# Up products with joined convolution rows, last rows by ScalarE, down weights issued ahead, and low parts shared four to three between GpSimd and VectorE

## The chip, the cores and the metric

The kernel runs on one core of a Trainium2 chip, in one launch. TensorE multiplies, VectorE, ScalarE and GpSimd do elementwise work, and SyncE (SP) issues most of the DMA transfers. The metric is the device time in microseconds, as the median of some runs; lower is better.

## What is computed

One layer of a decoder for 512 prompt tokens and 8 sequences of 8 sample tokens, 576 columns T in all, 2048 features, in fp32. The change lies in its last part, the gated MLP with a causal convolution of three taps over the tokens:

```python
def _ffn(u_hist, lp):
    uc = _dwconv_valid(u_hist, lp['w_dw_f'], lp['b_dw_f'])     # 3 taps a channel, 2 * 5632 channels
    gate, val = jnp.split(uc, 2, axis=-1)
    return jnp.dot(jax.nn.silu(gate) * val, lp['w_down'])

    u = jnp.dot(h2, lp['w_up'])                                # 2048 -> 2 * 5632
    u_hist = jnp.pad(u, ((0, 0), (FFN_CONV_W - 1, 0), (0, 0))) # a sample sequence: its saved rows
    y = x1 + gt2 * _ffn(u_hist, lp)
    return y, (k, v, ki, a_hist[:, -(CONV_W - 1):], u_hist[:, -(FFN_CONV_W - 1):])
```

The last two rows of u of each sequence are outputs too.

## The kernel before

Every fp32 matrix product is made of three fp32r products: a weight tile is split into a high part (ScalarE rounds it, `whi`) and a low part (the weight less the high part, `wlo`), the other operand as well (`XH`, `XL`), and TensorE adds high × high, high × low and low × high. A matmul takes a 128 x 128 weight and 288 columns (`TH`, half of T).

**Up loop.** The 44 pairs of channel tiles (gate and value; `FT` = 44) go in order. The first two pairs are ordinary products. The other 42 (`NU`) are the turns of a loop in which two inner halves by two halves of the columns by two channel tiles are made with seven products instead of eight (a Strassen-like scheme), from sums and differences of the weight blocks (`add_forms` 1 to 4, on VectorE, into `sums` and `raw`) and of the operand (four forms, `b11` to `b22`, made once on VectorE, split by `form_rows` on ScalarE and `form_lo` on VectorE). Turn i makes pair f = i + 2. A product p has two halves h of four weight tiles, 12 matmuls each.

For each half, ScalarE's `form_hi` writes `whi`, then a low part follows, then TensorE's `product`. There are four half buffers, so the high part of a half waits until TensorE is done with the half four before it. Before the change GpSimd makes the low parts of products 0, 2, 3, 5 and 6 (`POOL_LO`, two pieces of 256 columns a half, L925) and adds `u2` at the end (L929); VectorE makes those of products 1 and 4 (`DVE_LO`, L2595, 512 columns at once). The result of a pair comes from the seven products by adds on VectorE (`late_sum`, `gate_rows`, `value_rows`), with copies by ScalarE (`snap`), into rows `up` (prompt, two zero columns ahead) and `us` (sample, two saved rows ahead of each sequence).

**Convolution.** ScalarE makes the first tap with the bias (`taps`, L1272 prompt, L1273 sample), VectorE the other two (`conv3`, L2553 to L2558, prompt and sample apart), with copies of the last rows between (L2555, L2556). ScalarE applies silu, VectorE multiplies gate and value (`gate`, L2566), and the product goes to DRAM (`g_far`). A pair's convolution runs in the turn after its products.

**Loads.** SP's queue loads four raw blocks of 512 KB a turn, in the order 3, 2, 0, 1 (`block`), each when its slot is free. After the last turn four blocks of down weights, the residual `x1T` (in two pieces) and the first gated tiles `g32` are loaded the same way, and the down loop follows: 88 units of 48 matmuls, with low parts by GpSimd (L933) and `residual` on VectorE.

Each engine runs its instructions in the order in which the code is written; waits are semaphores.

## Time and profile before

| | us |
|---|---|
| median of 3 runs | 3043.79 (3033.14 to 3053.01) |
| profiled execution | 3037.9 |
| its span, first to last instruction | 3035.6 |
| TensorE busy in the span | 2802.8 (92%) |
| VectorE, ScalarE, GpSimd busy | 1986.6, 1081.7, 1688.1 |
| up loop after its first turn | 1457 to 2445 |

A row of the page's first part gives an engine's busy time, its share and its instructions. A row by stage gives the busy time of each engine in a stretch. A row of a timeline or of the chain gives start, duration, engine and line; in brackets how long the engine sat idle before it and who released it. A row of one line gives the fastest, the median and the slowest duration of its instructions. PE is TensorE, DVE VectorE, ACT ScalarE, POOL GpSimd.

### The profile page before, as it was taken

The page shows a single profiled execution, that of the slowest core. Times are in us where ns is not written, and L with a number is a line of the kernel's source. Part 1 is how long each engine was busy: PE and PEld are TensorE (multiplying, and loading weights), DVE is VectorE, ACT ScalarE, POOL GpSimd, SP SyncE. Part 2 cuts the span into 40 slices and gives each one's busy share as a digit, 9 for nine tenths or more (in the row PEclk, how much of TensorE's full clock was granted, in tenths as well). Part 3 has the DMA queues.
Part 4 walks back from the last instruction along what each step waited for, and adds up shares of the span by engine and source line. Part 5 has one row for each costly group of instructions (what it writes and reads, how often), then busy time and mean ns, then how long its engine had stood idle before and what let it go on. Part 6 is the DMA issues. An engine that isn't in the chain of part 4 may idle for free.

```text
span 3035.6 us, 52988 instructions
## 1 busy us (share of the span) xinstructions
PE 2802.8 (92%) x20368; PEld 2537.7 (84%) x20368; DVE 1986.6 (65%) x3277; ACT 1081.7 (36%) x1924; POOL 1688.1 (56%) x1936
## 2 busy tenths in 40 slices
PE   5798899999989779988999999999999989999999
PEld 2296588889955559988999999999999989999998
DVE  2225379999867542238898889888888854444442
ACT  2212323332125331226445555555555532121212
POOL 0134344443330254457888888888888854545453
PEclk9899999999989989999999999999999999999999
DMA  9822155552268763341333333333333353332323
GB/s 291 272 80 80 51 178 172 182 160 60 78 202 291 223 213 116 114 133 39 96 108 106 101 97 96 100 101 108 105 101 97 97 201 115 99 112 97 115 84 97
DMA packets 473891, 391.94 MB, mean 129 GB/s; under 512 B 29385, under 2 KB 402789, under 8 KB 473061
## 3 DMA queue, kind: packets, MB, share of 16 engines
q1 hardware_dynamic: 462882, 363.24, 39.1%
q0 software_dynamic: 8704, 19.27, 2.0%
q10 hardware_dynamic: 2075, 6.34, 0.7%
q8 instruction: 147, 2.41, 0.3%
q14 instruction: 83, 0.67, 0.1%
HBM read 363.85 MB, written 25.66 MB: 128 GB/s over the span
## 4 chain that ended last, share of the span: by engine, by line
PE 57%; POOL 20%; DVE 12%; issue 4%; DMA 3%; ACT 2%; ACTq 0%; SPq 0%; POOLq 0%; DVEq 0%
PE ps L1973 16%; POOL wlo L925 16%; PE ps L1425 16%; PE ps L2005 14%; DVE yb L2271 3%; DVE ye L2274 3%; DMA raw<-in_w_ada 2%; PE ps L1459 2%; POOL wlo L933 2%; DVE prod L2255 1%; POOL u L929 1%; ACT whi L1290 1%; DVE scP L2182 1%; PE ps L1837 1%; PE ps L1591 1%
## 5 line engine op out<-in xcount | busy, mean ns | idle before, releaser
L925 POOL TENSOR_TENSOR wlo<-raw,whi 128x256 fp32r<-128x256 f32 x672 | 707.7, 1084 | 103.5 <-ACT whi L1290 103.5
L876 POOL TENSOR_TENSOR wlo<-raw,whi 128x256 fp32r<-128x256 f32 (+1 forms) x424 | 350.1, 856 | 491.0 <-ACT whi L978 491.0
L2005 PE MATMUL ps<-XH,whi 128*128 128x288 f32 x1344 | 404.4, 301 | 56.3 <-POOL wlo L925 56.3
L933 POOL TENSOR_TENSOR wlo<-raw,whi 128x256 fp32r<-128x256 f32 x352 | 274.7, 812 | 295.8 <-ACT whi L1314 295.8
L1425 PE MATMUL ps<-XH,whi 128*128 128x288 f32 (+1 forms) x1760 | 390.4, 303 | 7.4 <-POOL wlo L876 6.0
L2005 PE MATMUL ps<-XH,wlo 128*128 128x288 f32 x1344 | 396.9, 295 | 0.0
L2005 PE MATMUL ps<-XL,whi 128*128 128x288 f32 x1344 | 396.8, 295 | 0.0
L2005 PE MATMUL ps<-x1R,whi 128*128 128x288 f32 x1344 | 395.6, 294 | 0.0
L1425 PE MATMUL ps<-XL,whi 128*128 128x288 f32 (+1 forms) x1760 | 379.0, 296 | 0.0
L1425 PE MATMUL ps<-XH,wlo 128*128 128x288 f32 (+1 forms) x1760 | 378.6, 297 | 0.0
L1290 ACT ACTIVATE whi<-raw 128x512 fp32r<-128x512 f32 x420 | 264.1, 629 | 235.2 <-PE ps L2005 223.1
L2481 DVE TENSOR_TENSOR yS<-ps,adaT 128x64 f32<-128x64 f32 x192 | 42.9, 224 | 421.9 <-PE ps L1973 330.3
L2005 PEld LDWEIGHTS ps<-XH,whi 128*128 128x128 f32 x1344 | 252.6, 188 | 74.8 <-issue 47.6
L1425 PEld LDWEIGHTS ps<-XH,whi 128*128 128x128 f32 (+1 forms) x1760 | 283.6, 190 | 26.7 <-issue 15.1
L978 ACT ACTIVATE whi<-raw 128x1024 fp32r<-128x1024 f32 (+1 forms) x106 | 111.0, 1051 | 525.5 <-PE ps L1425 358.9
L1425 PEld LDWEIGHTS ps<-XH,wlo 128*128 128x128 f32 (+1 forms) x1760 | 284.7, 190 | 0.0
L1425 PEld LDWEIGHTS ps<-XL,whi 128*128 128x128 f32 (+1 forms) x1760 | 284.2, 189 | 0.0
L2005 PEld LDWEIGHTS ps<-x1R,whi 128*128 128x128 f32 x1344 | 255.5, 190 | 0.0
L2005 PEld LDWEIGHTS ps<-XL,whi 128*128 128x128 f32 x1344 | 253.1, 188 | 0.0
L1314 ACT ACTIVATE whi<-raw 128x1024 fp32r<-128x1024 f32 x88 | 93.5, 1062 | 447.6 <-PE ps L1973 436.8
L2005 PEld LDWEIGHTS ps<-XH,wlo 128*128 128x128 f32 x1344 | 252.2, 188 | 0.0
L1459 PE MATMUL ps<-raw,sums 128*32 128x512 f32 x768 | 152.3, 671 | 37.9 <-DMA raw<-in_w_ada 37.7
(384 smaller groups left out, 6369.1 us busy)
## 6 DMA issues: line engine op xcount, KB each, us to landing
raw<-in_w_ada SPq DMA_DIRECT2D x192, 512.0 KB, 4.8
raw<-in_w_up SPq DMA_DIRECT2D x176, 512.0 KB, 4.2
raw<-in_w_down SPq DMA_DIRECT2D x88, 512.0 KB, 3.4
raw<-in_w_in SPq DMA_DIRECT2D x68, 512.0 KB, 5.6
Vp<-in_cache_v POOLq DMA_DIRECT2D x128, 128.0 KB, 3.9
raw<-in_w_out SPq DMA_DIRECT2D x32, 512.0 KB, 3.9
raw<-in_cache_k SPq DMA_DIRECT2D x64, 128.0 KB, 2.3
g32a<-g_far SPq DMA_DIRECT2D x6, 1152.0 KB
```

Of the source, the lines that this page charges most:

```text
L876: last = G.tensor_tensor(l[:, a:a + width // 4], raw_of(u, m)[:, a:a + width // 4], h[:, a:a + width // 4].bitcast(F32), ALU.subtract)
L925: last = G.tensor_tensor(lp[:, a:a + 256], src[:, a:a + 256], hp[:, a:a + 256].bitcast(F32), ALU.subtract)
L933: last = G.tensor_tensor(wlo[:, d % 2, a:a + 256], raw[:, d % 4, a:a + 256], whi[:, d % 2, a:a + 256].bitcast(F32), ALU.subtract)
L978: A.activation(parts(u, m)[0][:, 0:width], raw_of(u, m)[:, 0:width], ACT.Copy)\
L1290: A.activation(w_half(whi, i, p, h), form_of(p)[:, h * 512:h * 512 + 512], ACT.Copy).then_inc(s_hi, 1)
L1314: A.activation(whi[:, d % 2, :], raw[:, d % 4, :], ACT.Copy).then_inc(s_hi, 1)
L1425: ins = mm(dst[:, t, :], wt, x(k0 + k, t), start=st, stop=sp_)
L1459: ins = mm(ps_all[g:g + 32, bk, :], csT[:, kt, :], raw[:, s, kt % 2 * 512:kt % 2 * 512 + 512], start=kt < 4, stop=kt >= KT - 4)
L1973: ins = mm(pair(2 if nn else 6)[:, t, :], wt, x[g % 2][:, k, t * TH:t * TH + TH], start=k == 0 and wt is hp and x is gH, stop=k == GT - 1 ...
L2005: ins = mm(dst, wt, x(4 * h + k), start=h + k == 0 and wt is a and x is xh, stop=h == 1 and k == 3 and wt is b)
L2271: STT(even, hist[:, k:k + SEQ], w_tap(i, k), even, ALU.mult, ALU.add).then_inc(s_pe_, 1)
L2274: STT(odd, hist[:, k:k + SEQ], w_tap(i, k), odd, ALU.mult, ALU.add).then_inc(s_po, 1)
```

## The change

The prompt and sample rows of a channel tile now lie in one row `cin` of 594 columns, and the convolution's result in one row `conv` of 592, so that each tap is one instruction over all of it (the columns between sequences are computed and not used). The copies of the last rows go from VectorE to ScalarE. VectorE also makes product 6's low parts and the `u2` add; GpSimd keeps products 0, 2, 3 and 5. The four operand forms stand behind the first pair's convolution and gate. After the last turn the four blocks of down weights are issued ahead of `x1T`, which is loaded in four pieces.

```diff
-        POOL_LO, DVE_LO = (0, 2, 3, 5, 6), (1, 4)
+        POOL_LO, DVE_LO = (0, 2, 3, 5), (1, 4, 6)
...
+        CV = 2 + SEQ + DB * (2 + DS)
+        cin = at(o_f, "cin", [128, 2, CV])
+        up = cin[:, :, 0:2 + SEQ]
+        us = cin[:, :, 2 + SEQ:].rearrange("p v (b t) -> p v b t", b=DB)
+        conv = [four[:, v * CV:v * CV + CV - 2] for v in range(2)]
...
             last = NU - 1
             g_in(0, product_done(last, 1))
-            block(NU, 0)
-            sp.wait_ge(*product_done(last, 3))
+            for s in (3, 2, 0, 1):
+                block(NU, s)
+            for a in range(4):
+                x1_in(a, product_done(last, 4))
+                if a == 0:
+                    g_out(FT - 2)
             g_in(1, product_done(last, 3))
-            x1_in(1, product_done(last, 3))
-            block(NU, 1)
-            x1_in(0, product_done(last, 4))
-            block(NU, 2)
-            block(NU, 3)
-            g_out(FT - 2)
...
-                pool.wait_ge(*s_q.at(i + 1))
-                pool.wait_ge(*s_snap.at(2 * i + 2))
-                G.tensor_tensor(u2[:, :], u2[:, :], p5[:, :], ALU.add).then_inc(s_u4.sem, 1)
...
             def taps(f, v):
                 ch = f + v * FT
-                if v == 1:
-                    w(act, s_gt, f)
+                w(act, s_gt, f)
                 bias, tap = vT[:, 2, ch:ch + 1], vT[:, 5, ch:ch + 1]
-                A.activation(tmp[:, v, 0:SEQ], up[:, v, 0:SEQ], ACT.Identity, bias=bias, scale=tap)
-                A.activation(by8(tmp[:, v, SEQ:T]), us[:, v, :, 0:DS], ACT.Identity, bias=bias, scale=tap).then_inc(s_t0, 1)
+                A.activation(conv[v], cin[:, v, 0:CV - 2], ACT.Identity, bias=bias, scale=tap).then_inc(s_t0, 1)
+                last_rows_of(f, v)
+
+            def last_rows_of(f, v):
+                g, j, par = f // GT, f % GT, f // GT % 2
+                if j == 0:
+                    w(act, s_fot, g - 1)
+                A.activation(uS[:, par, v * GT + j, :].rearrange("p (b r) -> p b r", r=2), us[:, v, :, DS:], ACT.Copy)
+                A.activation(uP[:, par, v * GT + j, :], up[:, v, SEQ:], ACT.Copy).then_inc(s_us.sem, 1)
...
-                link.hold(STT(pa, up[:, v, 1:1 + SEQ], tap(1), pa, ALU.mult, ALU.add))
-                link(STT(sa, us[:, v, :, 1:1 + DS], tap(1), sa, ALU.mult, ALU.add))
-                V.tensor_copy(uS[:, par, v * GT + j, :].rearrange("p (b r) -> p b r", r=2), us[:, v, :, DS:])
-                V.tensor_copy(uP[:, par, v * GT + j, :], up[:, v, SEQ:])
-                STT(pa, up[:, v, 2:2 + SEQ], tap(2), pa, ALU.mult, ALU.add)
-                STT(sa, us[:, v, :, 2:2 + DS], tap(2), sa, ALU.mult, ALU.add).then_inc(s_c3, 1)
+                link(STT(conv[v], cin[:, v, 1:CV - 1], tap(1), conv[v], ALU.mult, ALU.add))
+                STT(conv[v], cin[:, v, 2:CV], tap(2), conv[v], ALU.mult, ALU.add).then_inc(s_c3, 1)
...
-                TT(gout[f % 2], sq[:, 0, :], tmp[:, 1, :], ALU.mult).then_inc(s_gt, 1)
+                TT(gout[f % 2][:, 0:SEQ], conv[0][:, 0:SEQ], conv[1][:, 0:SEQ], ALU.mult)
+                TT(by8(gout[f % 2][:, SEQ:T]), sample[0], sample[1], ALU.mult).then_inc(s_gt, 1)
...
                     TT(up[:, 0, 2:2 + TH], p1[:, :], bank(7, 128, 0, TH), ALU.add).then_inc(s_c11.sem, 1)
+                    TT(u2[:, :], u2[:, :], p5[:, :], ALU.add).then_inc(s_u4.sem, 1)
...
             conv3(0, 0)
             conv3(0, 1)
             gate(0)
+            operand_forms()
             add_forms(0, 1)
...
                 late_sum(i)
                 gate_rows(i)
+                lo(i, 6)
                 gate(f - 1)
                 if i < NU - 1:
                     add_forms(i + 1, 1)
...
-            for a in range(2):
-                dve.wait_ge(*s_x1i[a].at(16))
             for g in range(NG):
                 for n in range(16):
+                    if g == 0 and n % 4 == 0:
+                        dve.wait_ge(*s_x1i[n // 4].at(16))
```

On VectorE, the stretch of a turn from the gate rows to the two weight sums for products 3 and 2, before (`wlo<-sums` here is product 1's low part, `tmp` and `sq` the convolution's rows):

```order
L2612 TENSOR_TENSOR up<-up,ps 128x288
L2566 TENSOR_TENSOR rstd<-sq,tmp 128x576
L2575 TENSOR_TENSOR sums<-raw 128x1024
L2618 TENSOR_TENSOR up<-p1,ps 128x288
L2595 TENSOR_TENSOR wlo<-sums,whi 128x512 x2
L2622 TENSOR_TENSOR up<-u2,ps 128x224
L2623 TENSOR_TENSOR us<-u2,ps 128x8x8
L2579 TENSOR_TENSOR raw<-raw 128x1024
L2583 TENSOR_TENSOR raw<-sums,raw 128x1024
```

And in the changed kernel, with `four` for the convolution's rows:

```order
L2612 TENSOR_TENSOR cin<-cin,ps 128x288
L2595 TENSOR_TENSOR wlo<-sums,whi 128x512 x2
L2565 TENSOR_TENSOR four<-four 128x512
L2566 TENSOR_TENSOR four<-four 128x64
L2575 TENSOR_TENSOR sums<-raw 128x1024
L2618 TENSOR_TENSOR cin<-p1,ps 128x288
L2619 TENSOR_TENSOR u2<-u2,p5 128x288
L2595 TENSOR_TENSOR wlo<-sums,whi 128x512 x2
L2623 TENSOR_TENSOR cin<-u2,ps 128x224
L2624 TENSOR_TENSOR cin<-u2,ps 128x8x8
L2579 TENSOR_TENSOR raw<-raw 128x1024
L2583 TENSOR_TENSOR raw<-sums,raw 128x1024
```

Product 6's two low parts have come in ahead of the gate, the gate is two instructions, and `u2` stands ahead of product 1's low parts.

In SP's queue, from the last up weights to the down loop's first loads, before:

```order
L804 DMA g32a<-g_far 128x4x576
L792 DMA raw<-in_w_down 128x4x256
L804 DMA g32b<-g_far 128x4x576
L809 DMA x1T<-x1_far 128x8x576
L792 DMA raw<-in_w_down 128x4x256
L809 DMA x1T<-x1_far 128x8x576
L792 DMA raw<-in_w_down 128x4x256 x2
L797 DMA g_far<-sq 128x576
```

And in the changed kernel:

```order
L807 DMA g32a<-g_far 128x4x576
L795 DMA raw<-in_w_down 128x4x256 x4
L812 DMA x1T<-x1_far 128x4x576
L800 DMA g_far<-four 128x576
L812 DMA x1T<-x1_far 128x4x576 x3
L807 DMA g32b<-g_far 128x4x576
```

All four weight blocks stand ahead of `x1T` now, and `g32b` behind it.

## Rows read from the trace of the kernel before

**Rows 1.** The page, part 1: busy us, share of the span, instructions.

```profile
PE 2802.8 (92%) x20368; PEld 2537.7 (84%) x20368; DVE 1986.6 (65%) x3277; ACT 1081.7 (36%) x1924; POOL 1688.1 (56%) x1936
```

**Rows 2.** By stage, up loop: length, busy PE, PEld, DVE, ACT, POOL, clock, DMA.

```profile
1457.00:2445.00 988.00, 936.56 (x6905) 918.51 (x6904) 882.46 (x1188) 506.15 (x962) 868.25 (x860) 1.00 0.35 103
```

**Rows 3.** The chain that ended last, down stage: start, us, what.

```profile
2642.88 44.70 PE ps L1973 x336
```

**Rows 4.** The chain that ended last, one turn of the up loop.

```profile
1941.60 9.84 PE ps L2005 x72
...
1952.16 5.40 POOL wlo L925 x6
...
1958.26 1.94 POOL wlo L925 x2
1960.20 0.77 POOL u L929
```

**Rows 5.** The products' line: what TensorE sat idle for, us and times.

```profile
  POOL wlo L925: 85.6, 128
```

**Rows 6.** Single lines: instructions, fastest/median/slowest ns, first and last start.

```profile
L2554 DVE SCALAR_TENSOR_TENSOR tmp<-us,vT,tmp x88: 267/755/764, 1400.2 to 2456.8; 128x64 f32<-128x64 f32 x88
...
L2555 DVE COPY uS<-us x88: 174/611/618, 1400.9 to 2457.1; 128x16 f32<-128x16 f32 x88
...
L2595 DVE TENSOR_TENSOR wlo<-sums,whi x84: 683/1086/1292, 1428.6 to 2422.6; 128x512 fp32r<-128x512 f32 x84
...
L925 POOL TENSOR_TENSOR wlo<-raw,whi x672: 719/1179/3037, 1422.1 to 2437.8; 128x256 fp32r<-128x256 f32 x168
```

**Rows 7.** Timeline of VectorE, one turn: start, us, instruction, idle time before.

```profile
1936.25 1.72 DVE L2575 TENSOR_TENSOR sums<-raw 128x1024 f32<-128x1024 f32 x1 [0.73 <-POOL wlo L925]
...
1940.87 0.38 DVE L2622 TENSOR_TENSOR up<-u,ps 128x224 f32<-128x224 f32 x1
...
1944.22 1.23 DVE L2553 SCALAR_TENSOR_TENSOR tmp<-up,vT,tmp 128x512 f32<-128x512 f32 x1
...
1951.36 1.22 DVE L2588 TENSOR_TENSOR sums<-raw 128x1024 f32<-128x1024 f32 x1
...
1957.34 0.45 DVE L2607 TENSOR_TENSOR up<-u,ps 128x288 f32<-128x288 f32 x1
1957.83 0.39 DVE L2610 TENSOR_TENSOR up<-up,p 128x224 f32<-128x224 f32 x1
...
1958.76 0.85 DVE L2566 TENSOR_TENSOR sq<-sq,tmp 128x576 f32<-128x576 f32 x1
```

**Rows 8.** Timeline of ScalarE, the same turn.

```profile
1948.81 0.20 ACT L1279 ACTIVATE us<-sF 128x16 f32<-128x16 f32 x1
...
1956.97 0.68 ACT L1325 ACTIVATE sq<-tmp 128x576 f32<-128x576 f32 x1 [1.69 <-DVE tmp L2558]
...
1958.77 1.31 ACT L1290 ACTIVATE whi<-raw 128x512 fp32r<-128x512 f32 x2 [0.58 <-DMA raw<-in_w_up]
```

**Rows 9.** Timelines of VectorE and TensorE ahead of the up loop.

```profile
1390.10 2.99 DVE L2530 TENSOR_TENSOR x1T<-x1T 128x2304 f32<-128x2304 f32 x1
...
1399.12 1.11 DVE L2553 SCALAR_TENSOR_TENSOR tmp<-up,vT,tmp 128x512 f32<-128x512 f32 x1
...
1409.87 1.20 DVE L2566 TENSOR_TENSOR sq<-sq,tmp 128x576 f32<-128x576 f32 x1
1419.58 1.23 DVE L2575 TENSOR_TENSOR sums<-raw 128x1024 f32<-128x1024 f32 x1 [8.50 <-DMA raw<-in_w_up]
...
1399.83 0.58 PE L1425 MATMUL ps<-XH,whB 128*128 128x288 f32 x1 [7.09 <-POOL wlB L876]
```

**Rows 10.** Timelines of TensorE and ScalarE where the down stage begins.

```profile
2449.09 0.82 PE L1973 MATMUL ps<-gHa,whi 128*128 128x288 f32 x2 [3.70 <-POOL wlo L933]
...
2462.33 0.82 PE L1973 MATMUL ps<-gHa,whi 128*128 128x288 f32 x2 [5.35 <-DVE x1T L2485]
...
2458.35 1.06 ACT L1314 ACTIVATE whi<-raw 128x1024 fp32r<-128x1024 f32 x1 [3.87 <-DMA raw<-in_w_down]
```

49 lines of the change are left out of this document (22 added, 27 removed).

## The prediction

> **What bounds the kernel now.** I read the busy shares and slices of the page first, then the busy time by stage, then the chain of waits inside the longest stage. Over the span TensorE is busy 92% of the time and no other engine comes near [rows 1]. By stage it is the up loop that counts: 1457 to 2445 us, 988 us for its last 41 turns (turn 0 ends at about 1457), so 24.1 us a turn, and the granted clock there is 1.00 [rows 2]. In the down stage TensorE is fed without a pause. A row of the chain there gives its pace: 44.70 us for 336 matmuls of 288 columns, 0.133 us each [rows 3]. A turn of the up loop has 168 such matmuls (7 products of two halves, 12 matmuls a half), 22.35 us. So 24.1 - 22.35 = 1.75 us of a turn is waiting, and 41 × 1.75 = 72 us is all that this loop can give.
>
> The chain through one turn says who is waited for [rows 4]: GpSimd subtracts the low part of product 6, adds u2, subtracts four pieces for product 0 of the next turn, and only then TensorE runs 72 matmuls in a row. In the list of TensorE's waits at this line GpSimd's low parts hold 85.6 us [rows 5]. GpSimd is busy 868 of 988 us [rows 2], 21.1 us a turn, and what it does not use is its own wait for the high parts.
>
> The durations of single instructions show a second thing. The same VectorE instruction on 64 columns takes 0.27 us at its fastest and 0.755 at the median; a GpSimd piece of 256 columns 0.72 and 1.18 [rows 6]. Each stays the longer by about one instruction of the other: VectorE and GpSimd hold each other up where both read SBUF, one instruction for one. A tiny instruction therefore costs VectorE as much waiting (0.49 us) as a large one. The Trainium skill (SBUF — State Buffer, section "SBUF: two separate sides") says this as a rule: the shared ports are an exclusive lock, and the loser blocks for the winner's whole instruction. The trace agrees, with the two medians just given. Without such a lock the first chain below would cost its low figure and the time would be the first rival's.
>
> **GpSimd's part.** Of its 21 instructions a turn it loses five: four pieces of product 6 and u2. By the chain that is 1.94 + 0.77 us plus two of the six pieces that take 5.40 [rows 4]: about 4.5 us off the engine that is waited for. 16 pieces at 1.18 are 18.9 us, under 22.35 even when all are held up. GpSimd's sum stops being the bound; the time until one given piece is done still can be.
>
> **VectorE's part.** It loses, for each of the two rows of channels, two 64-column taps (0.755 each) and the copy of 16 columns (0.61): 2 × 2.12 = 4.2 us a turn [rows 6]; the copies of 2 columns I leave uncounted. It gains 80 columns on each of four taps: 0.08 each from the fastest times of 512 and 64 columns (0.683 - 0.267 over 448), 0.3 together; two low parts, 0.68 alone and 1.09 at the median, 1.4 to 2.2; the u2 add, as a 224-column add of two SBUF tiles (0.39 [rows 7]) alone, 0.9 held up; the gate cut in two, 0.27 to 0.755 more. In all 2.4 to 4.2 us. From 882/41 = 21.5 us busy [rows 2] that leaves 19.7 to 21.5: no bound by sum either.
>
> ScalarE gains two copies a channel row and loses the 64-column tap; at 506 of 988 us busy [rows 2] it has room. The copies follow each tap in its order; a copy of 16 columns takes it 0.20 us [rows 8], so the next high part comes up to 0.25 us later, or no later where the tap that goes pays for them. New waits: the first row's tap now waits for the gate of the pair before, with ScalarE's high parts queued behind it; that gate is half a turn old by then, so I count nothing. The waits for x1 move into the down loop, one for each four tiles, behind loads that are cut in four; nothing either.
>
> **Which wait ends last next.** Two chains run round a turn and come back to TensorE. I hold them against the halves that TensorE has meanwhile. Nine halves are 108 × 0.133 = 14.36 us; the last result of a half is out 0.26 us later than the next half begins (9.84 us for 72 matmuls [rows 4] less 72 × 0.133), which leaves 14.1.
>
> Chain A begins when product 4 ends and must feed half 2 of product 2 of the next turn. VectorE, in its new order: the four value sums at L2607 to L2612, 1.42 (from L2607's start to the gate's [rows 7]); product 6's two low parts, 1.3, as GpSimd has nothing to do just then; the gate in two pieces, 1.7 (1.05 alone, 1.9 held up); the sum for product 1, 1.7 (1.72 [rows 7]; 1.2 alone); L2618, 0.4; u2, 0.5; product 1's low parts, 1.3 (2.2 at the median; GpSimd is now done with product 0 earlier); the last value rows and the two sums at L2579 and L2583, 3.35 (from 1940.87 to 1944.22 [rows 7]); then the two taps, each behind a GpSimd piece of product 2, 1.3 each (1.23 and 0.08); GpSimd's last piece 0.6, its start overlapped. Sum 14.9, against 14.1: 0.7 to 0.8 us short. Unheld, with 1.2 for a sum of 1024 columns and 0.8 for a tap, it is 1.42 + 1.3 + 1.05 + 1.2 + 0.4 + 0.4 + 1.3 + 0.43 + 2.4 + 1.6 + 0.72 = 12.2 and hides. Held up by each of the eight GpSimd pieces that can lie in it, it is 8 × 0.49 = 3.9 more, less the 0.49 of the last, which holds nobody: 15.7 at most.
>
> Chain B begins when product 2 ends and must feed the second half of product 0: high part 0.71 with ScalarE's 0.25 ahead of it, low part 0.69, the sum for product 6 (L2588) 1.22, and then block 0 of the next weights, which is issued behind that sum: 1952.58 to 1958.77, 6.2 us, the high part waiting for the DMA [rows 7, 8]. Then 0.71 and four GpSimd pieces, 2.9 alone or 4.7 at the median: 12.7 to 14.5, against the same 14.1. So it lies between 1.4 in hand and 0.4 short; alone it would give a little less than chain A.
>
> I take chain A's 0.7: the turn goes from 24.1 to 22.35 + 0.7 = 23.05, and TensorE's wait moves from product 0 to product 2 (or partly stays at product 0's second half). 41 turns × 1.05 = 43 us.
>
> **Into the loop.** VectorE's four operand forms now stand behind the first channel pair's taps and gate. Before, they held GpSimd's pieces up, 3.0 us for a pair of form and piece, and TensorE idled 7.09 us for them until 1399.83 [rows 9]. That goes. But the forms then meet the next eight pieces instead, and all four first loads of the loop wait in SP's queue for the last of these (VectorE sat 8.50 us for them before [rows 9]). By the same 3.0 us a pair I place this last piece so: the two pairs of taps and the gate took 1399.12 to 1411.07 before, 12 us, of which some 4.5 are small instructions and hold-ups that go; 7.5 us from about 1393.7 (1 us after TensorE's stop at 1392.74) is 1401; four forms held up at 3.0 and two more pieces at 0.72 end at 1414.5. Before, the last piece must have been out by 1419.58 less a load's 5 to 6 us (the 6.2 of chain B), so about 1414 too: nothing gained there. So the idle time moves and I count 0; both ends are +2 and -6.
>
> **Out of the loop.** Two idle stretches, 3.70 and 5.35 us [rows 10]. In the second ScalarE waited 3.87 us for the third block of down weights, whose load stood in SP's queue behind those of x1 (4.7 MB) and g. Now the four blocks stand ahead of x1. The high part of that block then no longer waits for its load but for its buffer, which TensorE frees when it stops at 2456.98; it began at 2458.35 [rows 10]. That is 1.1 us with a signal's time, and the first stretch may give 0.5 as GpSimd comes free sooner, though VectorE's subtraction for g starts later. 1.5 us; ends 0 and 6.
>
> **The sum.** The profiled execution took 3037.9 us (span 3035.6 and 2.3 around it): 3037.9 - 43 - 0 - 1.5 = 2993. The runs of before have their median 6 us above this execution and lie 10 us to either side of it, so runs of after at 2990 to 3000 would be the same statement.
>
> **Rivals.** First, both chains hide (chain A between 12.2 and 14.1): the floor, 22.35 to 22.5 a turn, 41 × 1.7 = 70 us, 2964 with the same ends. For it: GpSimd has five instructions less, so fewer VectorE instructions are held up than before. Against: my placing of the pieces meets a hold-up at nearly every large VectorE instruction.
>
> Second, the hold-ups are nearly complete: chain A 15.1 to 15.7, the turn 23.35 to 23.95, a gain of 6 to 31 us with the 1.5, 3005 to 3030; 3018 in the middle. For it: VectorE was busy 882 of 988 us [rows 2], and much of that was hold-up. Against: only eight pieces lie in the chain.
>
> Third, on the other side: VectorE's order becomes the bound. Product 6's low part now stands in VectorE's row between the value sums and the gate; it waits for ScalarE's high part, which stands behind the silu, which waits for VectorE's own second pair of taps. Whatever is late there delays the gate, the next turn's sums and both chains. VectorE needs 21.5 us if all is held up and waited 2.6 us a turn before (24.1 less 21.5); the same wait on top of it gives 24.1, and from there on it decides. With 3.7 us of waits the turn is 25.2: 41 × 1.1 = 45 us slower, 3083. Against: 2.3 us of small instructions go from each pair of taps, and ScalarE's silu waited only 1.69 us for the second pair before [rows 8].
>
> Fourth, low part 6 only changes hands: TensorE waits for VectorE at product 6 as long as it waited for GpSimd at product 0, and the time stays 3038. The value sums (1.42) and one low part (0.69) take 2.1 us, and TensorE still works two halves there, 3.19 less 0.26, so I see little for it.
>
> **Chances.** My forecast (turn 22.65 to 23.35, 2977 to 3005) 0.52; the floor 0.20; nearly complete hold-ups 0.18; VectorE the bound 0.06; unchanged 0.04. Two in ten left out give 2958 (the floor and the start's 6 us) to 3022; the likeliest case alone is 2977 to 3005. A measurement of this kernel tells about 1% from no change, 30 us. Faster by more than that, below 3013 from the median of 3044: 0.52 + 0.20 + a third of 0.18 = 0.78; within: 0.12 + 0.04 = 0.16; slower 0.06.
>
> **What the profile would show.** Right: turns of 23 us in the chain; GpSimd's pieces no longer followed by u2; TensorE's wait at product 2 or at the second half of product 0, with VectorE's sums or taps and the w_up load ahead of it; VectorE busy about 20.5 us a turn; no 7 us gap at 1393 but one of similar size before 1431; the load of the third down block landing before TensorE wants it. Wrong: waits at product 6 on VectorE's L2595, a turn over 23.6, or no wait at all.

## The result and the profile after

| | before | after |
|---|---|---|
| median of the runs, us | 3043.91 (3033.14 to 3053.01, 4 runs) | 3009.77 (3004.04 to 3014.29, 4 runs) |
| ratio, 95% interval | | 0.9888 (0.9851 to 0.9925) |
| profiled execution, us | 3037.9 | 3004.0 |
| its span, us | 3035.6 | 3001.9 |

The forecast was 2993 with a range of 2958 to 3022. The time lies 17 us above the forecast, inside the range, and the kernel is 1.1% faster.

The first part of the page of after answers [rows 1] (busy us, share of the span, instructions):

```profile
PE 2803.3 (93%) x20368; PEld 2536.7 (85%) x20368; DVE 1915.1 (64%) x3095; ACT 1080.0 (36%) x2012; POOL 1528.7 (51%) x1726
```

TensorE does the same work; VectorE is busy 71.5 us less and GpSimd 159.4 us less. The row by stage for the up loop, cut as in [rows 2] (length, busy PE, PEld, DVE, ACT, POOL, clock, DMA share, GB/s):

```profile
1457.71:2413.61 955.90, 937.98 (x6910) 919.20 (x6908) 816.87 (x1028) 505.25 (x1045) 711.15 (x654) 1.00 0.36 107
```

The 41 turns take 955.9 us where they took 988, so a turn is 23.3 us. VectorE is busy 816.87 / 41 = 19.9 us of it (21.5 before), GpSimd 17.3 (21.2 before). What TensorE sits idle for at the line of the products, the first turn included (us, times), beside [rows 5]:

```profile
  POOL wlo L926: 66.0, 128
```

This row adds up matmuls and weight loads, which the profile counts as two engines, PE and PEld. The matmuls' waits alone, of after and of before (us, times, the longest):

```profile
PE ps L2008 <- POOL wlo L926: 27.2, 45, 4.9
PE ps L2005 <- POOL wlo L925: 57.3, 84, 2.4
```

So GpSimd's low parts are still what ends last, with about half of the matmuls' idle time. The chain through one turn of after, beside [rows 4] (start, us, what):

```profile
1919.19 1.29 DVE wlo L2595 x2
...
1921.54 0.76 DVE rstd L2566
1922.30 1.71 DVE sums L2575
1924.09 0.12 ACT whi L1294
...
1924.63 0.61 ACT whi L1294
...
1926.17 0.20 ACT uS L1276
1926.37 0.09 ACT uP L1277
1926.47 0.54 ACT whi L1294
1927.07 5.36 POOL wlo L926 x4
1932.47 8.51 PE ps L2008 x60
```

Before, the chain ended in GpSimd's pieces for product 0, and TensorE then ran 72 matmuls. Now it starts with product 6's low part on VectorE, goes through the gate (L2566) and the sum for product 1 (L2575), then through **ScalarE**: product 1's high parts, the first tap and its two copies of last rows (L1276, L1277), product 2's high part. Product 2's weights are a raw block as it was loaded: no sum of VectorE's feeds them. (The two sums at L2579 and L2583 make the weights of products 4 and 3, not 3 and 2 as the section on the change has it.) GpSimd's four pieces for product 2 take 5.36 us, and TensorE starts product 2's second half at 1932.47. Beside those pieces VectorE and GpSimd work as follows in after (timelines of the two; the third column is the engine), the place of [rows 7]:

```profile
1926.47 1.21 DVE L2579 TENSOR_TENSOR raw<-raw 128x1024 f32<-128x1024 f32 x1
1927.72 1.65 DVE L2583 TENSOR_TENSOR raw<-sums,raw 128x1024 f32<-128x1024 f32 x1
1929.29 1.31 DVE L2555 SCALAR_TENSOR_TENSOR four<-cin,vT,four 128x592 f32<-128x592 f32 x1
1930.63 1.20 DVE L2556 SCALAR_TENSOR_TENSOR four<-cin,vT,four 128x592 f32<-128x592 f32 x1
1932.68 0.98 DVE L2595 TENSOR_TENSOR wlo<-raw,whi 128x512 fp32r<-128x512 f32 x1 [0.85 <-ACT whi L1294]
1935.03 1.16 DVE L2595 TENSOR_TENSOR wlo<-raw,whi 128x512 fp32r<-128x512 f32 x1 [1.37 <-ACT whi L1294]
```

```profile
1927.07 8.56 POOL L926 TENSOR_TENSOR wlo<-raw,whi 128x256 fp32r<-128x256 f32 x8 [2.47 <-ACT whi L1294]
```

GpSimd makes eight pieces without a pause, four for product 2 and four for product 3, each beside a sum, a tap or a low part of VectorE. In the turn shown TensorE waits 0.65 us at product 2's second half, 0.14 at product 3's first, and the two halves behind those waits run 0.1 us longer each. (These waits are counted from one matmul's start to the next one's, less 0.133; the profile's idle time is shorter, since the records of matmuls overlap.) It waits nowhere else: at products 0, 1, 4, 5 and 6 the low part is 0.5 us or more ahead of its half in the two turns read.

**Where the 33.7 us of span came from.** I cut both traces at the same matmuls.

| stretch | before | after | difference |
|---|---|---|---|
| up to the end of the stage's first part on TensorE | 1392.7 | 1390.5 | -2.3 |
| from there to turn 1's first product | 63.8 | 67.25 | +3.4 |
| 41 turns | 988.7 | 955.8 | -32.9 |
| last up product to the second return of TensorE | 17.1 | 14.8 | -2.3 |
| the rest | | | +0.3 |

The first row has nothing to do with the change: in the five runs below that have the forms at their old place this moment lies between 1386.4 and 1397.2 us, with the same code ahead of it. So one execution's time carries some us from there, and I compare loops by the turn's length: the mean of 40 turns in the profiled execution, 24.14 us before and 23.31 after.

### The profile page after: what moved, and what is told of

It reads as the page before. It is cut to its first block, busy times and chain, and to the rows that moved or that the text cites. A ratio compares the mean times of both kernels' runs of the same rounds, so it can differ in the third digit from the quotient of the medians.

```text
span 3001.9 us, 52583 instructions
## 1 busy us (share of the span) xinstructions
PE 2803.3 (93%) x20368; PEld 2536.7 (85%) x20368; DVE 1915.1 (64%) x3095; ACT 1080.0 (36%) x2012; POOL 1528.7 (51%) x1726
## 4 chain that ended last, share of the span: by engine, by line
PE 57%; DVE 19%; POOL 11%; issue 6%; ACT 4%; DMA 3%; ACTq 0%; SPq 0%; DVEq 0%; POOLq 0%
PE ps L1976 17%; PE ps L1428 17%; PE ps L2008 12%; POOL wlo L926 8%; DMA raw<-in_w_ada 3%; PE ps L1462 2%; DVE yb L2274 2%; DVE ye L2277 2%; DVE sums L2575 2%; ACT whi L1294 2%; DVE wlo L2595 2%; POOL wlo L931 2%; POOL wlo L877 1%; DVE prod L2258 1%; DVE scP L2185 1%
## 5 line engine op out<-in xcount | busy, mean ns | idle before, releaser
L926 POOL TENSOR_TENSOR wlo<-raw,whi 128x256 fp32r<-128x256 f32 x672 | 735.4, 1125 | 259.0 <-ACT whi L1294 259.0
L877 POOL TENSOR_TENSOR wlo<-raw,whi 128x256 fp32r<-128x256 f32 (+1 forms) x424 | 359.4, 878 | 486.2 <-ACT whi L976 486.2
L931 POOL TENSOR_TENSOR wlo<-raw,whi 128x256 fp32r<-128x256 f32 x352 | 276.3, 816 | 296.9 <-ACT whi L1318 296.9
L1428 PEld LDWEIGHTS ps<-XH,whi 128*128 128x128 f32 (+1 forms) x1760 | 282.7, 189 | 30.6 <-issue 15.7
```

What stands on the lines that cost most here:

```text
L877: last = G.tensor_tensor(l[:, a:a + width // 4], raw_of(u, m)[:, a:a + width // 4], h[:, a:a + width // 4].bitcast(F32), ALU.subtract)
L926: last = G.tensor_tensor(lp[:, a:a + 256], src[:, a:a + 256], hp[:, a:a + 256].bitcast(F32), ALU.subtract)
L931: last = G.tensor_tensor(wlo[:, d % 2, a:a + 256], raw[:, d % 4, a:a + 256], whi[:, d % 2, a:a + 256].bitcast(F32), ALU.subtract)
L1428: ins = mm(dst[:, t, :], wt, x(k0 + k, t), start=st, stop=sp_)
```

## The experiments

My theory before the runs: VectorE and GpSimd hold each other up, and the chain through VectorE's sums and taps makes GpSimd's pieces for products 2 and 3 late. Rivals: VectorE's order as a whole is the bound; ScalarE's high part of product 2, which stands behind the first tap, comes late; block 0's transfer is late. Twelve kernels, all of them changes to after. Times are medians of the runs; each ratio is taken to runs of before made together with that kernel, whose medians lie between 3039.2 and 3043.9 us.

| run | turn, us | time, us | ratio to before, 95% interval |
|---|---|---|---|
| before | 24.14 | 3043.9 | |
| after | 23.31 | 3009.8 | 0.9888 (0.9851 to 0.9925) |
| low6_pool | 23.60 | 3023.4 (one run) | |
| split_rows | 23.91 | 3032.4 (one run) | |
| lo512 | 23.75 | 3023.0 | 0.9939 (0.9920 to 0.9958) |
| tap_apart | 23.11 | 2999.5 | 0.9866 (0.9834 to 0.9897) |
| hi_ahead | 23.36 | 3011.6 | 0.9908 (0.9872 to 0.9944) |
| p3_dve | 23.37 | 3004.1 | 0.9876 (0.9852 to 0.9899) |
| p3_taps_behind | 23.74 | 3023.8 | 0.9948 (0.9927 to 0.9969) |
| p3_order | 23.07 | 2995.5 | 0.9859 (0.9838 to 0.9879) |
| p3_order_hi | 22.37 | 2968.4 | 0.9769 (0.9752 to 0.9785) |
| p3_order_taps | 22.64 | 2979.7 | 0.9812 (0.9785 to 0.9839) |
| sp_order | 23.31 | 3017.0 (one run) | |
| ends_undone | 23.31 | 3010.3 (one run) | |

### What the two halves of the change are worth: low6_pool and split_rows

Product 6's low part and u2 go back to GpSimd:

```diff
-        POOL_LO, DVE_LO = (0, 2, 3, 5), (1, 4, 6)
+        POOL_LO, DVE_LO = (0, 2, 3, 5, 6), (1, 4)
```

> The changed kernel, with product 6's low part and the addition of u2 given back to GpSimd; the joined rows, the early down weights and the ends of the stage stay. If the third low part on VectorE is worth what the prediction says, GpSimd's pieces of product 0 are late again (fourteen 1.18-1.19 us pieces... ten halves of two pieces and an addition make about 21 us behind VectorE, and block 0's transfer before them): TensorE waits at product 0 again, 1.0-2.0 us a turn, and the turn is 23.6 to 24.1 us, the time 3022 to 3042 us. If VectorE's own chain alone sets the turn (its work falls by two low parts and an addition, some 2.3 us), the turn is at most that of the changed kernel, 23.3 us or less, and the time 3010 us or less.

The turn is 23.60 us, and the chain is that of [rows 4] again:

```profile
1925.03 4.78 POOL wlo L926 x5
...
1930.63 1.89 POOL wlo L926 x2
1932.52 0.77 POOL u L930
1933.28 4.68 POOL wlo L926 x4
...
1938.01 9.84 PE ps L2011 x72
```

So the wait is back at product 0, as expected. Product 0's four pieces take what they took before (4.68 us and 4.66). What has become shorter is the stretch from product 5's first piece to product 6's second half: 5.6 us (1925.03 to 1930.63) against 6.1 (1952.16 to 1958.26). The joined rows alone are worth 24.14 - 23.60 = 0.54 us a turn, the third low part with u2 another 0.29 on top.

The other half alone: product 6 stays on VectorE, the taps are cut into prompt and sample rows and VectorE copies the last rows, as before the change:

```diff
-                link(STT(conv[v], cin[:, v, 1:CV - 1], tap(1), conv[v], ALU.mult, ALU.add))
-                STT(conv[v], cin[:, v, 2:CV], tap(2), conv[v], ALU.mult, ALU.add).then_inc(s_c3, 1)
+                link.hold(STT(pa, up[:, v, 1:1 + SEQ], tap(1), pa, ALU.mult, ALU.add))
+                link(STT(sa, us[:, v, :, 1:1 + DS], tap(1), sa, ALU.mult, ALU.add))
+                V.tensor_copy(uS[:, par, v * GT + j, :].rearrange("p (b r) -> p b r", r=2), us[:, v, :, DS:])
+                V.tensor_copy(uP[:, par, v * GT + j, :], up[:, v, SEQ:])
+                STT(pa, up[:, v, 2:2 + SEQ], tap(2), pa, ALU.mult, ALU.add)
+                STT(sa, us[:, v, :, 2:2 + DS], tap(2), sa, ALU.mult, ALU.add).then_inc(s_c3, 1)
```

> The changed kernel, with the convolution's second and third taps cut into prompt and sample rows again, and the last rows copied by VectorE; product 6's low part stays on VectorE. By the theory that VectorE and GpSimd hold each other up instruction for instruction, four sample taps and four copies a turn come back, each of up to 0.6-0.75 us whatever its size: VectorE's chain to product 2's second half grows by two sample taps and two copies (1.5 to 2.6 us), and the turn is 24.5 to 26 us, the time 3060 to 3120 us, slower than before the change. By the theory that columns set the price (the same columns in all, four short instructions at 0.15-0.25 us each), the chain grows by 0.6 to 1.0 us, the turn is 23.9 to 24.3 us, the time 3035 to 3052 us.

The single instructions cost what the theory says: 0.755 us for 64 columns and 0.612 for 16 at the median (line: fastest/median/slowest ns), and only the copy of 2 columns stays at 0.155:

```profile
L2560 DVE SCALAR_TENSOR_TENSOR four<-cin,vT,four x88: 272/755/765, 1400.9 to 2447.0; 128x64 f32<-128x64 f32 x88
L2561 DVE COPY uS<-cin x88: 174/612/618, 1401.2 to 2447.3; 128x16 f32<-128x16 f32 x88
L2562 DVE COPY uP<-cin x88: 153/155/716, 1401.3 to 2447.4; 128x2 f32<-128x2 f32 x88
```

But the turn is 23.91: below the range of the first theory, whose durations came, and at the lower end of the second's, whose durations did not. The row by stage says why:

```profile
1458.90:2439.38 980.48, 958.97 (x6910) 923.05 (x6908) 970.53 (x1356) 478.25 (x881) 689.33 (x655) 1.00 0.35 104
```

VectorE is busy 970.53 of 980.48 us (99%), 23.67 of a turn of 23.91. The small instructions add 3.75 us of work a turn to the 19.92 of after; 3.4 us of that goes into what VectorE had idle, and only the rest lengthens the turn. I had added them to the chain as if nothing in it were waiting. So here VectorE's order is the bound, the third rival of the forecast. This half of the change alone (the first tap stays joined on ScalarE, the gate cut in two) is worth 24.14 - 23.91 = 0.23 us a turn.

### How the two engines hold each other up: lo512

One subtraction of 512 columns a half on GpSimd instead of two of 256:

```diff
-                        for a in (0, 256):
-                            last = G.tensor_tensor(lp[:, a:a + 256], src[:, a:a + 256], hp[:, a:a + 256].bitcast(F32), ALU.subtract)
-                        last.then_inc(s_lo, 1)
+                        G.tensor_tensor(lp, src, hp.bitcast(F32), ALU.subtract).then_inc(s_lo, 1)
```

> The changed kernel, with each half's low part on GpSimd made by one subtraction of 512 columns instead of two of 256. In the trace of the changed kernel a 256-column piece takes 0.73 us beside an idle VectorE and 1.2 us beside a working one; a VectorE subtraction of 512 columns grows from 0.68 to 1.22 us and the 0.22 us sample gate to 0.76 us when a piece runs beside it, 0.54 us each, whatever their own size. If the hold-up is a fixed price for each instruction, it stays at 0.54 us on VectorE, a half on GpSimd costs 1.4 + 0.5 = 1.9 us instead of 2.4 us, the waits at products 2 and 3 go, and the turn is 22.4 to 22.7 us, the time 2972 to 2985 us. If the two engines take turns, each for as long as the other's instruction works, the same VectorE instructions grow by about 1.08 us (the sample gate to 1.3 us), a half costs 2.0 to 2.5 us, and only the order changes: the turn is 22.9 to 23.5 us, the time 2993 to 3018 us.

First after, then lo512, for the sample gate (fastest/median/slowest ns of 64 columns) and GpSimd's pieces:

```profile
L2566 DVE TENSOR_TENSOR four<-four x22: 220/762/766, 1399.0 to 2410.6; 128x64 f32<-128x64 f32 x22
L926 POOL TENSOR_TENSOR wlo<-raw,whi x672: 723/1187/3039, 1421.5 to 2406.6; 128x256 fp32r<-128x256 f32 x168
```

```profile
L2564 DVE TENSOR_TENSOR four<-four x22: 211/1309/1317, 1402.2 to 2428.8; 128x64 f32<-128x64 f32 x22
L925 POOL TENSOR_TENSOR wlo<-raw,whi x336: 1277/1814/3606, 1424.7 to 2421.8; 128x512 fp32r<-128x512 f32 x168
```

The gate's 64 columns take 0.22 us alone, 0.76 beside a piece of 256 columns and 1.31 beside one of 512: 0.54 and 1.09 us more. So the price is not a fixed one for an instruction. It grows with the instruction that the other engine works on, and is 0.18 or 0.19 us less than that one takes at its fastest (0.723 and 1.277). The second theory of this run is right in VectorE's durations; GpSimd's half, 1.81 us at the median, is nearer the first's 1.9 than the second's 2.0 to 2.5. The second theory's turn (22.9 to 23.5) is not right either: 23.75 us, since VectorE's instructions that meet a piece are held up twice as long, and product 6's low part on VectorE becomes late (by 0.54 us in the turn read). Small pieces are the better ones here.

### Which wait makes product 2 late: tap_apart and hi_ahead

The third tap of the value rows goes into VectorE's idle time between the two halves of product 4's low part:

```diff
-                    conv3(f - 1, 1)
+                    tap_a(f - 1, 1)
...
-                lo(i, 4)
+                lo(i, 4, 0)
+                if i:
+                    tap_b(f - 1, 1)
+                lo(i, 4, 1)
```

> The changed kernel, with the third tap of the value rows of the pair before put between the two halves of product 4's low part, where VectorE stands idle 1.4 us a turn. By the theory that GpSimd's pieces for products 2 and 3 are late because VectorE's sums and taps run beside them, one tap of 0.6-0.7 us leaves that stretch: TensorE's wait at product 2's second half falls from 0.65 to 0-0.3 us, that at product 3 from 0.35 to 0-0.2 us, the turn is 22.4 to 22.8 us and the time 2972 to 2990 us. By the rival that VectorE's order as a whole is the bound, the moved tap delays the low part of product 4's second half, and with it the next chain: the turn stays at 23.2 to 23.6 us, the time 3005 to 3022 us. By the rival that ScalarE's high part of product 2 is what comes late, nothing changes at product 2: 23.3 us, 3008 to 3012 us.

Turn 23.11, 0.2 us less; that of my theory was 22.4 to 22.8. The wait at product 2's second half fell from 0.65 to 0.12 us as expected, but one of 0.48 came at product 3's second half. The timeline of GpSimd shows eight pieces as long as before (8.56 us in after):

```profile
1926.49 8.58 POOL L926 TENSOR_TENSOR wlo<-raw,whi 128x256 fp32r<-128x256 f32 x8 [2.47 <-ACT whi L1294]
```

Taking one VectorE instruction from beside product 2's pieces only put it beside product 3's.

On ScalarE, product 2's first high part goes ahead of the first tap and its copies:

```diff
-                    first_tap(f - 1, 1)
                     form_hi(i, 2, 0)
+                    first_tap(f - 1, 1)
```

> The changed kernel, with ScalarE's high part of product 2's first half ahead of the first tap of the pair before, not behind it. If that high part, which starts about 0.65 us after its buffer could take it, is what GpSimd's piece waits for, GpSimd's pieces of products 2 and 3 come 0.4-0.65 us earlier, the wait at product 2's second half falls from 0.65 to 0-0.25 us, and the turn is 22.6 to 22.9 us, the time 2980 to 2995 us. If the pieces are late through VectorE's sums and taps alone, they finish when those do: the turn stays at 23.2 to 23.4 us, the time 3003 to 3014 us. If the tap, coming 0.6 us later, delays VectorE, the turn grows to 23.5 to 23.9 us, the time 3018 to 3034 us.

The turn is 23.36, unchanged, as the second case had it, but not for its reason. Product 2's second half now has its low part 0.14 us early and TensorE does not wait there. It waits 0.67 us at product 3's first half and 0.14 at its second:

```profile
1928.85 9.54 POOL L926 TENSOR_TENSOR wlo<-raw,whi 128x256 fp32r<-128x256 f32 x8 [1.75 <-ACT whi L1294]
```

The eight pieces start earlier and take 9.54 us. In the chain of hi_ahead no VectorE instruction is left: it goes from TensorE's release of a half buffer through one high part and six of these pieces (7.70 us) to product 3. So both single edits heal the place that the forecast named, and the run of eight pieces, four halves in a row beside working VectorE instructions, keeps the turn within 0.2 us of where it was. TensorE uses up those four halves in 4 × 12 × 0.133 = 6.4 us.

### Taking product 3 out of the run of eight: p3_dve and what stood behind it

```diff
-        POOL_LO, DVE_LO = (0, 2, 3, 5), (1, 4, 6)
+        POOL_LO, DVE_LO = (0, 2, 4, 5), (1, 3, 6)
...
-                lo(i, 4)
+                lo(i, 3)
```

> The changed kernel, with product 3's low part on VectorE and product 4's on GpSimd (VectorE still makes three of seven). In the changed kernel GpSimd has eight pieces in a row for products 2 and 3, beside VectorE's sums and taps, and they take 8.6 us; TensorE's waits there are 0.65 us at product 2 and 0.35 us at product 3. If this run of eight pieces is the bound, product 3's wait goes and product 2's, which comes ahead of it, stays: the turn is 22.9 to 23.0 us, the time 2992 to 3000 us. If what binds is VectorE's chain to the taps, product 3's low part, which now stands behind them, is late: the turn is 23.3 to 24.0 us, the time 3008 to 3040 us.

TensorE waits neither at product 2 nor at product 3 any more (the low parts are 0.7 to 2.7 us early), but the turn is 23.37: it waits at product 0. The chain there:

```profile
1914.25 4.42 POOL wlo L926 x4
...
1918.68 0.37 SPq L795
...
1919.14 5.56 DMA raw<-in_w_up
...
1924.78 0.64 ACT whi L1294
...
1925.49 4.49 POOL wlo L926 x4
...
1930.03 5.04 PE ps L2008 x36
```

Product 4 is read from block 2's buffer, GpSimd now frees that buffer 2 us later against TensorE's use of it (the low part is 1.07 us ahead of its half, 3.02 in after), and SyncE issues block 0, which is wanted first, behind block 2. This is the forecast's second chain (block 0's transfer, then GpSimd's pieces for product 0), lengthened by a queue. (Counted from a turn's first product, block 2 is issued at 14.0 us here and at 12.4 in after; the 5 to 5.6 us that two expectations below name for this compare the times of two executions.) The same with the value rows' taps behind product 3's low part, product 2's high part ahead of the tap and the operand forms at their old place:

> The changed kernel with three things: product 3's low part on VectorE and product 4's on GpSimd; the value rows' two taps behind product 3's low part instead of ahead of it; product 2's first high part ahead of the first tap on ScalarE. Also the operand forms stand ahead of the first convolutions again, as before the change. If the wait in a turn is that of GpSimd's eight pieces for products 2 and 3 beside VectorE's sums and taps, then four pieces beside the two sums, started 0.65 us earlier, end 0.2 us or more ahead of TensorE's need, VectorE's product 3 is 1.5 us ahead of it, and no wait is left: the turn is 22.35 to 22.7 us, the start some 3 us shorter, the time 2967 to 2983 us. If VectorE's total work in its order binds, the taps come later and hold the sums for product 6 and the next turn's chain: the turn is 23.2 to 23.8 us, the time 3002 to 3030 us.

Turn 23.74: product 2's second half is 1.8 us early, and TensorE waits 1.3 and 0.5 us at product 0's first half in the two turns read (0.6 on average), for block 0, and 0.5 at its second. Both turns lie in the range of the case that blamed VectorE, but VectorE's low part of product 3 is 1.8 us or more early in both, and VectorE is busy only 772 of 973 us in the second. Both expectations failed by the same omission; neither theory had the queue of loads in it.

Then block 0 ahead of block 2 in SyncE's order, with the forms at their old place:

```diff
                 block(i + 1, 3)
-                block(i + 1, 2)
+                block(i + 1, 0)
...
-                block(i + 1, 0)
+                block(i + 1, 2)
                 block(i + 1, 1)
```

> The changed kernel with product 3's low part on VectorE and product 4's on GpSimd (as in the run of that alone), SyncE's issue of block 0 ahead of that of block 2 in each turn, and the operand forms ahead of the first convolutions again. In the run with products 3 and 4 exchanged alone, the waits at products 2 and 3 went (slack 0.7 to 1.7 us) and new ones stood at product 0 (0.35 and 0.52 us): there block 2's buffer came free 5.6 us later than in the changed kernel, since GpSimd reads it now, and block 0 is issued behind it (0.47 us after block 2, at 1942.31). If that queue is the cause, block 0 goes out some 3 us earlier, product 0's waits go, and what is left is the chain from product 4's end to product 2's second half, 14.3 to 14.5 us against TensorE's 14.35: the turn is 22.35 to 22.6 us, the start some 3 us shorter, the time 2960 to 2975 us. If product 0 waits for GpSimd's own pieces (which were held to 2.2 us a half there by VectorE's gate and sum), the turn stays at 23.1 to 23.4 us, the time 2995 to 3006 us.

Product 0's wait goes (0.85 us in hand), so the queue was its cause. But the turn is 23.07, since 0.65 us at product 2's second half is back, the wait of after to the hundredth: I had taken that chain's length from a run in which TensorE waited elsewhere first. With product 2's high part ahead of the tap as well:

> The same three edits, and ScalarE's high part of product 2's first half ahead of the first tap. In the run of that edit alone GpSimd's first piece for product 2 came 0.65 us earlier against product 4's end, and the wait went from product 2 to product 3, whose pieces stood behind. With product 3 on VectorE nothing stands behind it: no wait is left, the turn is 22.33 to 22.5 us, the time 2957 to 2970 us, 0 to 8 us below that of the three edits without this one. If the tap, now 0.6 us later, pushes VectorE's low part of product 3 or GpSimd's of product 4, the turn is 22.6 to 23.0 us, the time 2970 to 2990 us.

Turn 22.37, time 2968.4, 1.2% below after by the two ratios. Behind its first turn TensorE does not wait in the loop at all, and product 0's low parts still have 0.7 us or more in hand, so the queue was indeed what held them:

```profile
1448.39:2365.71 917.32, 917.32 (x6910) 916.89 (x6908) 840.17 (x1028) 497.17 (x1045) 744.13 (x654) 1.00 0.37 111
```

In these runs three edits are wanted together: product 3 off GpSimd's run, block 0 not behind block 2, and ScalarE's high part not behind the tap. Product 2's second half has 0.14 us in hand then. With the value rows' taps behind product 3's low part in addition:

> The four edits, and the value rows' two taps behind product 3's low part on VectorE instead of ahead of it. In the run of this without the new order of the blocks, product 2's second half had 1.8 us of slack, product 4's second half 0.07 us, since the taps now run beside GpSimd's pieces for product 4. If those pieces bind once product 0's wait is gone, the turn is 22.4 to 22.8 us, the time 2962 to 2982 us, no faster than with the taps ahead. If nothing binds, it is 22.33 to 22.4 us and 2957 to 2965 us.

Turn 22.64: as its first case had it, the taps now run beside GpSimd's pieces for product 4, and TensorE waits 0.3 us at product 5 in the second of the two turns read. No gain.

The control, the order of the blocks alone:

> The changed kernel with SyncE's issue of block 0 ahead of block 2's alone; products 3 and 4 and the start stay as in the changed kernel. There ScalarE's first high part of product 0 starts when its buffer comes free and TensorE does not wait at product 0 (slack 0.8 to 1.6 us), and block 2's buffer is free 5 us earlier than with product 4 on GpSimd: if the queue matters only through block 2's late buffer, nothing changes here: 23.2 to 23.4 us a turn, 3003 to 3014 us. If block 0's transfer was part of what binds, the turn falls by 0.2 us or more, the time to 2995 us or less.

Turn 23.31, so block 0's transfer has room in after, as the first case had it. Its time, 3017, lies above the range given; in this execution TensorE is 10 us later than in after when the loop begins (the row behind the wait of 3.03 us, shown below at 1413.10, stands at 1423.31), which comes from ahead of anything that the edit touches.

### The two ends of the stage: ends_undone

The operand forms stand ahead of the first convolutions again, and SyncE issues the down weights in the old order.

```diff
-            for s in (3, 2, 0, 1):
-                block(NU, s)
-            for a in range(4):
-                x1_in(a, product_done(last, 4))
...
+            block(NU, 0)
+            sp.wait_ge(*product_done(last, 3))
...
-            operand_forms()
```

> The changed kernel, with the two ends of the up stage as before the change: the operand forms ahead of the first convolutions, and SyncE's issues at the stage's end (down weights, g, residual rows) in the old order. The loop has not been touched: 23.3 us a turn. If the regrouped start costs the 3.4 us by which the stretch from TensorE's stop ahead of the stage to the loop's first product grew (63.8 to 67.25 us), that stretch is 63.5 to 64.5 us here, with TensorE's clock granted in full through the first product's halves. If the early down weights are what saves 2.3 us at the other end, the stretch from TensorE's last up product to its return is 16.5 to 17.5 us here, against 14.8 us, and the two cancel: time 3003 to 3015 us. If the start's length is only a shift of work from one stretch to the other, it stays at 66 to 68 us and the time is 3008 to 3018 us.

The start is 63.7 us, that of before the change. The other end is 17.7 us, a little above before's 17.1 and the expected 16.5 to 17.5. The turn is 23.31, and the time, 3010.3, is that of after. In after the start looks so, beside [rows 9] (timeline of TensorE, the rows behind its two longest waits):

```profile
1413.10 0.53 PE L1428 MATMUL ps<-XH,whi 128*128 128x288 f32 x2 [3.03 <-POOL wlo L877]
1424.58 0.58 PE L2008 MATMUL ps<-XH,whi 128*128 128x288 f32 x1 [4.87 <-POOL wlo L926]
```

The 7.09 us at 1399.83 are gone, and 3.03 and 4.87 have come. By stretch, of after (the clock is the number behind POOL's), the two stretches in which the granted clock is at the lower of its two levels, and the sum from TensorE's stop to the loop's second turn:

```profile
1422.10:1432.30 10.20, 6.21 (x24) 5.89 (x25) 9.54 (x8) 7.94 (x14) 7.61 (x6) 0.50 0.02 8
1442.60:1449.40 6.80, 6.28 (x27) 5.93 (x26) 3.72 (x4) 1.26 (x2) 4.92 (x5) 0.50 0.53 154
sum 67.25, PE 54.77 PEld 53.34 DVE 49.27 ACT 29.65 POOL 44.45; mean PE 10.95 PEld 10.67 DVE 9.85 ACT 5.93 POOL 8.89
```

and of before, where there is one such stretch:

```profile
1397.20:1404.00 6.80, 4.17 (x17) 4.20 (x18) 6.20 (x7) 0.50 (x1) 6.18 (x5) 0.50 0.00 0
sum 63.79, PE 50.80 PEld 49.93 DVE 48.36 ACT 30.38 POOL 46.90; mean PE 16.93 PEld 16.64 DVE 16.12 ACT 10.13 POOL 15.63
```

In both, TensorE makes the same matmuls. From its stop at 1392.74 to 1456.53 before, it is busy 50.8 us and idle 13.0. From 1390.46 to 1457.71 after, it is busy 54.8 us and idle 12.5. So TensorE doesn't wait longer; the same work takes 4.0 us more. Before, it stands 7.09 us, and the clock is at the lower level for 6.8 us, from within that stand. After, it stands 3.03 and 4.87 us, and the clock is at the lower level for 10.2 us, from within the second stand; it stands 1.51 us (until 1429.31) and 2.37 us (until 1441.37) in the loop's first turn, and the clock falls once more, for 6.8 us. Some halves there take 2.8 us from first to last start, instead of 1.46. TensorE is busy 12.5 us at that level, against 4.2 before. If a matmul there takes twice its time, half of the difference, 4.2 us, is what this costs; that is an estimate, and 4.0 is measured. In ends_undone the four stretches from 1397 have a clock of 0.81, 1.00, 0.89 and 0.96, and TensorE is busy 52.0 and idle 11.7 us.

The place of the operand forms does not settle this alone. With the forms behind the gate, as in after, the same stretch is 66.0 to 67.5 us in low6_pool, tap_apart, hi_ahead and sp_order, but 63.4 in p3_dve, 63.7 in lo512 and 60.4 in split_rows. p3_dve has the stands of 3.0 and 4.9 us too, and a clock at the lower level for 10.2 us, but not a second time; there the wait of 2.37 us in the loop's first turn is 1.78. So the 3.4 us are what the new start costs together with after's loop. What in the first turn decides about the second fall, no run takes apart.

The other end of the stage, beside [rows 10] (TensorE, then ScalarE):

```profile
2417.01 0.50 PE L1976 MATMUL ps<-gHa,whi 128*128 128x288 f32 x2 [3.40 <-POOL wlo L931]
2428.28 0.82 PE L1976 MATMUL ps<-gHa,whi 128*128 128x288 f32 x2 [4.70 <-DVE x1T L2488]
```

```profile
2423.68 1.06 ACT L1318 ACTIVATE whi<-raw 128x1024 fp32r<-128x1024 f32 x1 [6.19 <-PE ps L1976]
```

The high part of the third down block waits for TensorE, that is for its buffer, and no longer for the DMA; in ends_undone the chain leads through that block's load again. Behind the high part come ScalarE's last silu, VectorE's last gate and its residual (L2488), and then TensorE.

TensorE's two idle stretches are 3.40 and 4.70 us instead of 3.70 and 5.35, 0.95 us less (3.38 and 5.11 in ends_undone; 7.9 to 9.0 together in the eleven other runs that have the new order at this end). The other 1.3 of the 2.3 us in the table lie in the 48 matmuls between the two stretches. Of after and of before:

```profile
2417.01:2423.60 6.59, 6.58 (x48) 6.34 (x48) 3.90 (x4) 0.49 (x3) 4.57 (x4) 1.00 1.05 399
2449.09:2456.98 7.89, 7.88 (x48) 7.66 (x48) 3.71 (x8) 3.57 (x7) 3.29 (x4) 0.82 1.07 380
```

The granted clock was 1.00 there in the profiled execution of after, and 0.82 in that of before. In those eleven runs the way to the second return takes 16.2 to 17.3 us, not 14.8. So the early weights save up to 1.1 us of idle time; the rest of the 2.3 us is the clock in one execution.

## Why the prediction was right, and where it was off

**GpSimd's part** held. The wait at product 0 went, u2 is gone from the chain, and GpSimd is busy 17.3 us a turn against 18.9 forecast at 1.18 a piece. low6_pool brings the old chain back. (The 85.6 us that the forecast took from [rows 5] as TensorE's wait count matmuls and weight loads together; the matmuls' part is 57.3. No term of the sum rests on it.)

**VectorE's part** held: 19.7 to 21.5 us a turn forecast, 19.9 measured, and 20.5 named as the sign. That a tiny instruction costs a full hold-up was right in the durations of split_rows. The forecast called it "one instruction for one" at 0.49 us; lo512 shows that the price grows with the other's instruction, 0.54 us for 256 columns and 1.09 for 512. The Trainium skill (SBUF — State Buffer, section "SBUF: two separate sides") has it so, the loser blocking for the winner's whole instruction; the trace agrees, with those two numbers, but for the 0.18 or 0.19 us by which they fall short of the whole instruction.

**Chain A** was right in its place and in its first half, and wrong in its second. The wait at product 2's second half was forecast at 0.7 us and is 0.65. From product 4's last result to the end of the sum for product 1 the forecast has 1.42 + 1.3 + 1.7 + 1.7 = 6.1 us, and the trace 6.2 (1917.77 to 1923.99). From there the forecast goes on through VectorE's product 1, sums and taps, and counts one GpSimd piece, 0.6. None of these feeds product 2, whose weights are a raw block; they only hold GpSimd's pieces up while they run. The chain of after goes through ScalarE: product 1's high parts wait for that sum, then come the first tap and the two copies, then product 2's high part, and GpSimd's four pieces, 5.36 us. The step that failed is "The copies follow each tap in its order ... or no later where the tap that goes pays for them", after which no ScalarE instruction stands in chain A: ScalarE has time over the turn, but not just there. With ScalarE's high part ahead of the tap, product 2's second half is 0.14 us early instead of 0.65 late (hi_ahead and p3_order_hi). That the sum came out at the wait is therefore partly luck, with one route in place of another of nearly the same length (14.65 us in the trace, 14.9 forecast).

**The missing wait.** The turn is 23.31, not 23.05, because TensorE also waits at product 3, 0.14 us and two halves that run 0.1 longer. The forecast followed one piece to TensorE, the last one of product 2. Behind it stand product 3's four pieces on the same engine, and GpSimd gives a half in 8.56 / 4 = 2.1 us beside a working VectorE where TensorE uses one up in 1.6. p3_order, which takes product 3 from GpSimd, has a turn of 23.07 with the wait at product 2 left in. This term, 0.25 us a turn or 10 us in all, is the largest. The sum was made for the profiled execution: 2993 against 3004.0. Of the 11 us, 10 are this wait, 3.4 the start, -0.8 the other end, -2.3 lie ahead of the stage and 0.3 behind it. The median is another 5.7 us higher, as the median of before was by 6.

**Chain B** was rightly taken as no worse than chain A: product 0 had 0.5 us or more in hand in after, and the order of the blocks alone changes nothing. p3_dve shows how near it is: one load behind another, and it is the bound.

**Into the loop**: 0 forecast, with +2 and -6 as ends; +3.4 measured, outside. The forecast of the loads held: GpSimd's last piece ends at 1413.07 (1414.5 forecast), and the first sum starts at 1418.94 instead of 1419.58. "So the idle time moves and I count 0" held too, for the idle time: 12.5 us against 13.0. What the forecast left out is the clock. One long stand became two shorter ones, and the time at the clock's lower level grew from 6.8 to 17.0 us, which costs 4.0 us of TensorE's time. The old place of the forms gives most of it back (63.7 us in ends_undone, 62.0 in p3_order_hi), but so does a loop with another first turn (63.4 in p3_dve).

**Out of the loop**: -1.5 forecast with ends 0 and -6; -2.3 measured, of which 0.95 is idle time and 1.3 the clock of this execution. The step was right as told: the load had been the wait, and the buffer is now. Its size was 0.65 us in the second idle stretch (1.1 forecast) and 0.3 in the first (0.5).

**The rivals.** The floor did not come, since ScalarE's order and the run of eight pieces kept a wait; p3_order_hi reaches it, 22.37 a turn. (Its 2964 us are 2966 by the forecast's own terms, 3037.9 - 70 - 1.5.) The nearly complete hold-ups give a turn from 23.35 on, and 23.31 comes close; but chain A took 14.65 us, not the 15.1 to 15.7 of that rival, and the rest is the wait at product 3. VectorE the bound did not come either, but does in split_rows, where the small instructions are left in. The fourth did not come: product 6's low parts have 0.8 us in hand. The two parts of the change nearly add up: 0.54 us a turn by the joined rows alone, 0.23 by the third low part with u2 alone, 0.83 together.

## What to carry to other kernels

When two engines take turns at a memory, follow a chain through every engine that feeds it, at that place in the turn: an engine that is idle half the time still delays the chain if a tap and two copies stand ahead of the one instruction that is wanted. A wait that is cured at one product often stands at the next: look at the run of consecutive pieces that one engine must make against what TensorE uses up meanwhile, and give neighbouring products to different engines. And when an operand moves to another engine, look at the buffer that it frees and at what is queued behind that buffer's load.
